# Row normalisation of an mLSTM layer: square, root and scaling set in three places of the unit loop, scaling on GpSimd

## What is computed

```python
h_f, st_f = mlstm_scan(q, k, v, log_i[0], log_f[0], ...)
h_b, st_b = mlstm_scan(flip(q), flip(k), flip(v), ...)
hs = h_f + flip(h_b)
hs = hs * lax.rsqrt(jnp.mean(hs * hs, axis=-1, keepdims=True) + RMS_EPS)
hs = hs.transpose(0, 2, 1, 3).reshape(B, T, A_V).astype(h.dtype) * g_head
out = (hs * jax.nn.sigmoid(o)) @ w_out
```

## Time and profile before

| what | us |
|---|---|
| median of three runs | 2864.34 (2863.76 to 2868.72) |
| the profiled execution, its time | 2866.64 |
| its span | 2864.6 |
| busy: PE, DVE, ACT, POOL | 2562.6 (89%), 1171.4 (41%), 582.8 (20%), 257.5 (9%) |
| mean granted clock of TensorE, share of full speed | 0.955 |

### The profile page before, as it was taken

One profiled execution on the slowest core, in us unless ns is written; L12 is line 12 of the kernel. 1 busy time (PEld: TensorE's weight loads), 2 busy tenths in 40 slices (PEclk: granted clock), 3 DMA queues, 4 the chain that ended last, 5 costly groups with the idle time before them and its releaser, 6 DMA issues.

```text
span 2864.6 us, 63958 instructions
## 1 busy us (share of the span) xinstructions
PE 2562.6 (89%) x28913; PEld 2065.5 (72%) x28913; DVE 1171.4 (41%) x2013; ACT 582.8 (20%) x1016; POOL 257.5 (9%) x162
## 2 busy tenths in 40 slices
PE   5899868999999989978888888878699999999993
PEld 3566545577776757747777777766499999999992
DVE  4434657645454366636555656627200000000004
ACT  3101132200010010024444444430201110111001
POOL 0000230000000000003333222220100000000001
PEclk9999989999999989979999999999699999999996
DMA  8554102322211113310000000002355555655553
GB/s 324 231 231 171 45 1 95 133 74 74 74 70 61 76 53 120 110 53 4 22 22 22 23 22 22 6 5 89 125 211 199 191 206 203 221 186 200 204 198 121
DMA packets 52552, 322.00 MB, mean 112 GB/s; under 512 B 8160, under 2 KB 10336, under 8 KB 21600
## 3 DMA queue, kind: packets, MB, share of 16 engines
q1 hardware_dynamic: 41824, 281.23, 26.8%
q10 hardware_dynamic: 7040, 20.45, 2.0%
q0 software_dynamic: 3456, 16.78, 1.5%
HBM read 289.07 MB, written 29.36 MB: 111 GB/s over the span
## 4 chain that ended last, share of the span: by engine, by line
PE 83%; DVE 7%; ACT 4%; issue 3%; DMA 2%; POOL 1%; SPq 0%; POOLq 0%; ACTq 0%; DVEq 0%
PE PS L867 34%; PE PS L1506 16%; PE PS L1521 8%; PE PS L1122 3%; PE PS L1249 3%; PE PS L1241 2%; PE PS L845 1%; PE PS L1181 1%; PE PS L1231 1%; DMA arena<-in_k 1%; PE PS L1313 1%; PE PS L595 1%; PE PS L1208 1%; PE PS L1174 1%; ACT arena L1772 1%
## 5 line engine op out<-in xcount | busy, mean ns | idle before, releaser
L867 PE MATMUL PS<-arena,ring 128*128 128x320 f32 x2680 | 753.6, 440 | 40.3 <-DVE arena L2369 12.3
L867 PEld LDWEIGHTS PS<-arena,ring 128*128 128x128 f32 x2680 | 513.6, 193 | 267.5 <-issue 34.2
L1506 PE MATMUL PS<-arena,ring 128*128 128x192 f32 x2816 | 471.2, 331 | 3.2 <-ACT arena L1887 3.2
L1506 PEld LDWEIGHTS PS<-arena,ring 128*128 128x128 f32 x2816 | 468.9, 194 | 4.3 <-ACT arena L1887 4.1
L1521 PE MATMUL PS<-arena,ring 128*128 128x192 f32 x1408 | 230.1, 326 | 0.0
L1521 PEld LDWEIGHTS PS<-arena,ring 128*128 128x128 f32 x1408 | 229.0, 190 | 0.0
L2618 DVE TENSOR_TENSOR arena<-arena,PS 128x192 f32<-128x192 f32 x88 | 31.2, 355 | 444.3 <-ACT arena L1893 444.3
L867 PE MATMUL PS<-arena 128*128 128x320 f32 x536 | 151.1, 432 | 0.0
L867 PEld LDWEIGHTS PS<-arena 128*128 128x128 f32 x536 | 101.8, 190 | 42.4
L1249 PE MATMUL PS<-arena 64*64 64x64 f32 x3200 | 119.0, 219 | 10.5 <-issue 10.1
L786 POOL TENSOR_TENSOR arena<-arena,const 128x512 f32<-128x512 f32 (+1 forms) x24 | 26.2, 1091 | 1109.5 <-DVE arena L2470 776.1
(11 more groups left out here) (330 smaller groups left out, 3152.2 us busy)
## 6 DMA issues: line engine op xcount, KB each, us to landing
ring<-in_k SPq DMA_DIRECT2D x145, 1024.0 KB, 4.8
arena<-in_k SPq DMA_DIRECT2D x48, 1024.0 KB, 9.0
ring<-in_exd SPq DMA_DIRECT2D x32, 1408.0 KB, 5.9
ring<-in_ffd SPq DMA_DIRECT2D x8, 1408.0 KB, 6.1
rkv_s<-arena ACTq DMA_DIRECT2D x24, 320.0 KB, 4.1
expert_rows<-arena POOLq DMA_DIRECT2D x4, 1536.0 KB, 10.3
x<-in_x SPq DMA_DIRECT2D x2, 2560.0 KB, 9.3
arena<-expert_rows ACTq DMA_DIRECT2D x8, 512.0 KB, 4.3
```

The source lines that it names most:

```text
L867: m = pe.matmul(out, lhs[:, k], rhs[:, k], start=k == 0, stop=k == count - 1)
L1506: m = pe.matmul(PS[:, k % 4, t * CAP:(t + 1) * CAP], w[:, kt, t * P:(t + 1) * P], xe[:, kt], start=kt == 0, stop=kt == KT - 1)
```

## The change

`head_norm_rows` is split. sq of chunk n is issued by ScalarE after W of unit 2n + 3, ms by VectorE at the end of the same unit's turn, ln and rs by ScalarE after W of unit 2n + 4, and hn by GpSimd at the end of its turn for unit 2n + 4, as one multiplication of 128x1024 by a column broadcast over each head. Chunk 7 is thereby treated inside the loop too. Chunk 9 stays behind the loop; its hn is VectorE's. Ahead of the loop stands one preload of a table that holds both logarithm and exponential. TensorE's transposes wait for GpSimd or VectorE instead of ScalarE.

```diff
         n, hf = u // 2, u % 2
-        act += [f"W{u}"]
+        act += [f"W{u}"] + row_norm_act(u)
...
-        if n in SECOND and hf == 0:
-            dve += chunk_sum(n - 1)
-            act += chunk_act(n - 1)
+        if hf and n - 1 in SECOND:
+            dve += [f"ms{n - 1}"]
...
+        if hf == 0 and n - 2 in SECOND:
+            pool += [f"hn{n - 2}"]
     dve += unit_tail(NU - 1)
     pool += [f"add{NU - 1}"]
-    dve += chunk_sum(7)
-    act += chunk_act(7)
-    dve += chunk_sum(9)
-    act += chunk_act(9)
+    dve += ["ms9", "hn9"]
+    act += ["sq9", "ln9", "rs9"]
...
+def row_norm_act(u):
+    n, hf = u // 2, u % 2
+    if hf:
+        return [f"sq{n - 1}"] if n - 1 in SECOND else []
+    return [f"ln{n - 2}", f"rs{n - 2}"] if n - 2 in SECOND else []
...
+        rows_of_heads = lambda n: hs_t[:, MGRP[n][1]].rearrange("p (h n) -> p h n", h=AH)
...
+                if hf == 0 and n - 2 in SECOND:
+                    mact.wait(pool, f"rs{n - 2}")
+                    hh = rows_of_heads(n - 2)
+                    mpool.done(pool.tensor_tensor(hh, hh, ms[:, MGRP[n - 2][1]].unsqueeze(2).to_broadcast([P, AH, DV]), ALU.mult), f"hn{n - 2}")
...
-                mact.wait(pe, f"hn{n}")
+                (mdve if n == 9 else mpool).wait(pe, f"hn{n}")
...
-                mact.wait(act, f"rs{n}")
-                for h in range(AH):
-                    hh = hs_t[:, c, h * DV:(h + 1) * DV]
-                    i = act.activation(hh, hh, ACT.Copy, scale=ms[:, c, h:h + 1])
-                mact.done(i, f"hn{n}")
+            act.preload_act_table_set("natural_log_exp_and_others")
...
-                if n in SECOND and hf == 0 and n - 1 in SECOND:
-                    head_norm_rows(n - 1)
-            head_norm_rows(7)
-            head_norm_rows(9)
+                if hf and n - 1 in SECOND:
+                    square_rows(n - 1)
+                if hf == 0 and n - 2 in SECOND:
+                    root_rows(n - 2)
+            square_rows(9)
+            root_rows(9)
...
-                if n in SECOND and hf == 0 and n - 1 in SECOND:
+                if hf and n - 1 in SECOND:
                     square_sum(n - 1)
             unit_end(NU - 1)
-            square_sum(7)
             square_sum(9)
+            mact.wait(dve, "rs9")
+            mdve.done(dve.tensor_tensor(rows_of_heads(9), rows_of_heads(9), ms[:, MGRP[9][1]].unsqueeze(2).to_broadcast([P, AH, DV]), ALU.mult), "hn9")
```

More of the change, by code:

```diff
@@ L1641, in _, with square_rows @@
             finish_in(IN_SLABS - 1)
-            def head_norm_rows(n):
+            def square_rows(n):
                 c = MGRP[n][1]
@@ L1648, in head_norm_rows, with root_rows @@
                 mact.done(act.activation(sqt.rearrange("p h n -> p (h n)"), hs_t[:, c], ACT.Square), f"sq{n}")
+            def root_rows(n):
+                c = MGRP[n][1]
                 mdve.wait(act, f"ms{n}")
```

## The result

The changed kernel took 2834.72 us (median of four, 2828.35 to 2841.35) against 2864.05 us (four runs) for the kernel before; the ratio is 0.9902, with a 95% interval of 0.9884 to 0.9921. Two later comparisons gave 0.9914 (0.9899 to 0.9929) and 0.9901 (0.9879 to 0.9923). The forecast was 2837.0 us, in a range of 2833.0 to 2843.5. The profiled execution took 2833.83 us, its span is 2832.0 us.

A forecast was written before the change was run, and what follows sets the result against it. In units 10 to 16 of the mLSTM loop the bound was taken to be ScalarE's queue, not TensorE. Stall 24.7 plus tail 2.6 gave 27.3 us off 2864.34, so 2837.0 us, range 2833 to 2843.5.

The forecast's parts named there:

- The stall: mLSTM loop, W10 to W19: 63.47 us becomes nine units at 4.31 us, 38.8 us, giving back 24.7 us.
- Squares, logarithms and powers at no cost: ScalarE in the loop: squares end 0.6 to 0.8 us before the next masks, powers by + 3.7 of 4.31; cost 0.
- Sums in VectorE's idle time: VectorE after odd units' tails: each sum pushes P by 1.13 us into 1.16 us idle; taken as 0, at most 4.5.
- Scaling on GpSimd: GpSimd in the loop: a scaling takes 2.1 us, 2.5 at the dear end; cost 0.
- the limit of 4.1 us: GpSimd's queue in the loop: it holds without cost until one scaling costs some 4.1 us.
- the crossing at 11.2 us: GpSimd's scaling price from which the kernel is slower than before: 3 (x - 4.1) + (x - 5) = 27.3.
- the rival on the other side: Slower than before: dear GpSimd scalings delay additions, squares and exponentials; at 13 us per scaling 2871.7 us; chance 0.02.
- The tail: Behind the loop: chunk 7 is done inside it, so chunk 9's chain lets the products start 2.6 us earlier.
- The clock rival: P1 and P2 of the output projection: shorter TensorE idleness may hold the clock, 2.2 us more, 2834.8 us; chance 0.18.
- four scalings at 0 to 4.5 us: Alternative placement on VectorE: four instructions of about 1.2 us would need its 1.16 us gap, at 0 to 4.5 us.
- the table loads as part of the wait: ScalarE in the loop: ten table loads leave, their cost counted within the 63.47 us of W10 to W19.
- The total: Whole kernel: 24.7 + 2.6 = 27.3 us off the median of 2864.34 us, giving 2837.0 us; chance 0.63.

The follow-up runs named there:

- reordered kernel: Changed kernel with VectorE's products of chunks 4 to 7 ahead of chunk 9's sum, scaling and gs operations after the loop; ratios to the kernel before 0.9892 and 0.9878.

## Why the prediction was right

- **The stall.** 24.7 us forecast, 24.46 measured. The missing 0.24 is one W pace of 4.52 us (unit 15 to 16): VectorE idles 0.25 us ahead of h of unit 13, in this trace as in that of before. It is no wait on a moved step, since the kernel before has it, and it is absent where VectorE does the scalings; what it is stays open.
- **Squares, logarithms and powers at no cost.** Right; 0.70 and 0.92 us were left before the next W, where 0.6 to 0.8 and 0.6 had been counted.
- **Sums in VectorE's idle time.** Right; a margin of 0.18 us instead of 0.1. P was pushed by 1.0 us and not by 1.13, since the sum starts 0.13 us before P would have.
- **Scaling on GpSimd.** 2.1 us forecast by the row with the same broadcast, 1.90 measured. The slope behind the limit of 4.1 us held: 3 (x - 4.1) + (x - 5) gives 5.9 us at x = 5.8, measured 62.17 - 56.12 = 6.05; it gives 29.9 at 11.8, measured 29.7. So the crossing at 11.2 us, on which the rival on the other side rested, was sized right too. The limit itself is only bracketed: 3.8 us cost nothing, and no run lies between that and 5.8.
- **The tail.** 2.6 forecast, 2.63 measured, by the chain that was written down: the first product starts 413.32 - 400.88 = 12.44 us after W19, where 12.5 had been said. What the prediction did not ask is whether that chain had to be there: the reordered kernel took 4.95 us more off it up to P1.
- **The clock rival.** It did not come true: the granted clock fell again while TensorE idled, and P1 and P2 took 5.98, 6.63 and 7.63 us in the three profiles, against 6.60 and 6.52 before. TensorE's stretches of the first show where the clock fell:

```profile
413.00:414.00 1.00, 0.00 (x0) 0.00 (x0) 0.79 (x2) 0.00 (x0) 0.00 (x0) 1.00 0.95 401
414.00:415.00 1.00, 0.31 (x2) 0.34 (x3) 1.00 (x2) 0.00 (x0) 0.00 (x0) 0.52 1.00 418
```

  In the reordered kernel, where TensorE idled 2.33 us between the transposes and P1 and not 4.84 and then 1.36, the clock held in both profiles: 4.54 us.
- **What was sized wrong beside the sum.** The prediction said that VectorE would take four scalings at 0 to 4.5 us; it takes them at 2.1 us. Of that, three scalings that VectorE and GpSimd held up cost 0.52 us each in the loop, a mechanism that the prediction did not have, and 0.77 is the last one, which no idle time follows (0.2 comes back, since this run lacks the slow pace named above). And it spoke of the table loads as part of the wait without asking which of them lay on it: one in each pair was hidden behind the sum.
- **The total.** 27.3 us forecast from the stage, 26 to 29 us between the medians of the three comparisons; single executions scatter by several us in stages that the change does not touch. That the first median, 2834.72, lies beside the 2834.8 of the clock rival is chance: that rival's mechanism failed, and 29.3 - 27.1 = 2.2 us of the first difference lie outside the stage.

## What to carry to other kernels

An engine that is 20% busy can still set the pace if its work comes in one lump in front of what others wait for: cut the lump at its waits, and put each piece where the profile shows idle time on that engine just ahead of the next thing it must do. Spread like that, squares on ScalarE, sums on VectorE and scalings on GpSimd made the loop 0.2 us longer than its undisturbed pace. The table loads mattered little (1.3 of 27.1 us), and so did ScalarE or GpSimd for the scaling (0.2), but VectorE cost 2.1; so count first what a place costs, then what an instruction costs, and look at what the neighbouring engine does at that moment. Behind a loop, ask of each step in the chain whether the next consumer needs it: 5 of the tail's 17 us here were a chain ahead of products that did not need it.

## What the runs showed of the hardware that was not expected

- ScalarE's load of a table that belongs to a waiting instruction ran ahead of the wait: in the kernel before one went from 424.48 to 425.76 while its logarithm waited until 430.13, and for chunk 4, with the preload, the 1.28 us gave way to 1.29 us of idle time.

```profile
424.48 1.28 ACT L1650 ACT_TABLE_LOAD   x1
430.13 0.30 ACT L1650 ACTIVATE arena<-arena,const 128x8 f32<-128x8 f32 x1 [4.37 <-DVE arena L2218]
```

- A multiplication on VectorE with both inputs in SBUF and GpSimd's work held one another up: 2.00 us instead of 1.22, and 2.89 instead of 1.90, while VectorE's instructions with one input in PSUM were untouched.
- GpSimd's 128x1024 multiplication with a broadcast column, in place, took 1.90 us, less than twice the 1.04 us of the same form at 512 columns.
- The same instructions behind the first SiLU took 2310 to 2328 us from one execution to the next.
